# Slicing a mixer's LayerNorm and SiLU by tokens, and mixing a 31-tap convolution into its recurrence

## The reference

```
z = rmsnorm(x) @ w_in;  x_rnn, g_rnn, glu_a, glu_b = split(z, 4)          # 512 channels each
xr = conv4(x_rnn);      y_rnn = rg_lru_bidir(xr, ...) * gelu(g_rnn)       # scans over time, both ways
c = conv31(glu_a * sigmoid(glu_b));  c = silu(layernorm(c, ln_g, ln_b))   # over the 512 channels
x += concat(rmsnorm(y_rnn), rmsnorm(c)) @ w_out
x += softmax(q k^T) v @ w_xo
s = (rmsnorm(x) @ w_pq) . sub_keys      # 8 heads x 2 halves x 128 keys; top 16 of each, then of their 256 sums
x += sum_k gate_k * gelu(rmsnorm(x) . u_tab[idx_k]) * v_tab[idx_k]        # 128 picks a token
y = rmsnorm(x)
```

## Time and profile before

| | |
|---|---|
| median of three runs | 4637.21 us |
| the profiled execution | 4632.38 us, its span 4630.6 us |
| PE / DVE / POOL / ACT busy | 53% / 57% / 60% / 12% of the span |
| moved by DMA | 1497 MB, of it 1342 MB gathers |

### The profile page before, as it was taken

One profiled execution on the slowest core, in us unless ns is written; L12 is line 12 of the kernel. 1 busy time (PEld: TensorE's weight loads), 2 busy tenths in 40 slices (PEclk: granted clock), 3 DMA queues, 4 the chain that ended last, 5 costly groups with the idle time before them and its releaser, 6 DMA issues.

```text
span 4630.6 us, 30437 instructions
## 1 busy us (share of the span) xinstructions
PE 2465.1 (53%) x9492; PEld 984.2 (21%) x9492; DVE 2647.7 (57%) x5775; ACT 551.6 (12%) x1122; POOL 2763.9 (60%) x2585
## 2 busy tenths in 40 slices
PE   8996177956687444255355355355246345333354
PEld 7652132333242111011011011011012011000000
DVE  4427857688513557647657647656755755845400
ACT  6221313320210000000000000000010010000000
POOL 0003646736412366777777777777777777777754
PEclk9998588977888666577577577567668567655556
DMA  5334758969846697999999999999999999999987
GB/s 206 109 135 156 267 202 302 338 231 405 332 172 245 227 327 284 348 387 364 369 406 363 374 401 380 373 394 380 345 405 377 350 406 392 351 407 420 418 305 277
DMA packets 406466, 1496.99 MB, mean 323 GB/s; under 512 B 44576, under 2 KB 49056, under 8 KB 397856
## 3 DMA queue, kind: packets, MB, share of 16 engines
q0 software_dynamic: 368640, 1342.34, 76.6%
q1 hardware_dynamic: 31008, 144.30, 8.2%
q10 hardware_dynamic: 6656, 8.39, 0.5%
HBM read 1463.40 MB, written 31.46 MB: 323 GB/s over the span
## 4 chain that ended last, share of the span: by engine, by line
POOL 36%; PE 16%; DVE 16%; issue 14%; DMA 14%; ACT 3%; DVEq 1%; ACTq 0%; POOLq 0%; SPq 0%
POOL arena L572 20%; POOL arena L556 16%; DMA arena<-in_u,IDX 9%; DVE arena L1156 5%; PE ps L1521 4%; DMA arena<-in_v,IDXT 4%; PE ps L1640 3%; DVE arena L1087 3%; PE ps L1654 2%; PE ps L1691 2%; PE ps L1543 1%; PE ps L1556 1%; DVE arena L1205 1%; DVE CI L1211 1%; DVE CI L1202 1%
## 5 line engine op out<-in xcount | busy, mean ns | idle before, releaser
L556 POOL DMA_INDIRECT arena<-in_u,IDX x1280 | 1421.5, 1111 | 1198.5 <-DVE arena L1156 507.7
L1156 DVE SCALAR_TENSOR_TENSOR arena<-arena 128x1024 f32<-128x1024 f32 x1280 | 1546.3, 1224 | 1025.8 <-DMA arena<-in_u,IDX 1015.6
L1654 PE MATMUL ps<-arena,ZB 128*32 128x512 f32 x5120 | 1005.0, 926 | 1770.5 <-DMA arena<-in_v,IDXT 1765.2
L572 POOL DMA_INDIRECT arena<-in_v,IDXT x1280 | 1340.0, 1047 | 651.1 <-issue 381.3
L1654 PEld LDWEIGHTS ps<-arena,ZB 128*32 128x32 f32 x5120 | 200.2, 145 | 2488.1 <-issue 2471.2
L1691 PE MATMUL ps<-arena 128*128 128x512 f32 x1216 | 563.2, 619 | 13.3 <-DVE arena L1285 8.9
L1691 PEld LDWEIGHTS ps<-arena 128*128 128x128 f32 x1216 | 237.1, 200 | 356.8 <-issue 341.6
L1521 PE MATMUL ps<-arena 128*128 128x512 f32 (+1 forms) x768 | 284.0, 529 | 4.8 <-ACT arena L666 2.6
L863 ACT ACTIVATE ZB<-ACTT 128x4 f32<-128x4 f32 x320 | 58.5, 205 | 1786.7 <-PE ps L1654 1781.2
L1087 DVE SCALAR_TENSOR_TENSOR arena<-arena,cols 128x256 f32<-128x256 f32 (+1 forms) x240 | 212.2, 884 | 6.5
L1521 PEld LDWEIGHTS ps<-arena 128*128 128x128 f32 x768 | 145.7, 192 | 143.1 <-issue 134.4
(11 more groups left out here) (176 smaller groups left out, 1900.6 us busy)
## 6 DMA issues: line engine op xcount, KB each, us to landing
arena<-in_items SPq DMA_DIRECT2D x56, 1024.0 KB, 4.8
arena<-in_u,IDX POOLq DMA_INDIRECT x1280, 6.3
arena<-in_v,IDXT POOLq DMA_INDIRECT x1280
arena<-x_scratch SPq DMA_DIRECT2D x18, 512.0 KB, 6.7
arena<-in_w_out SPq DMA_DIRECT2D x16, 512.0 KB, 9.5
wp_scratch<-arena SPq DMA_DIRECT2D x2, 4096.0 KB, 17.8
arena<-wp_scratch SPq DMA_DIRECT2D x8, 1024.0 KB, 4.8
arena<-wp_scratch SPq DMA_DIRECT2D x2, 4096.0 KB, 30.4
```

The lines of the kernel that those rows point to most:

```text
L556: g.indirect_dma_start(out=u_slot[n % RU], out_offset=None, in_=a["u"], in_offset=bass.IndirectOffsetOnAxis(ap=IDX[b % 2][:, k:k + 1], axi ...
L572: g.indirect_dma_start(out=v_slot[group % VG * GROUP + quad], out_offset=None, in_=a["v"], in_offset=bass.IndirectOffsetOnAxis(ap=IDXT[b % ...
L1156: v.scalar_tensor_tensor(out=u_slot[n % RU], in0=u_slot[n % RU], scalar=1.0, in1=H[b % 2], op0=ALU.mult, op1=ALU.mult, accum_out=DOT[b % 2 ...
L1654: ins = t.matmul(ACC[b % 2][32 * quad:32 * quad + 32, half * BANK:(half + 1) * BANK], ZB[:, z + quad * ZW:z + quad * ZW + 32], v_slot[n % ...
```

## The change

`CHUNKS` puts the four g chunks ahead of the first b chunk. In both groups the taps go into the recurrence: after each step of `lru` and of the later `conv4`s up to three taps (`TAPS_EACH`) of channels already gated are issued, and what is left follows. LayerNorm and SiLU go by `SLICES` of tokens: the prompt is one slice, the sample five (128, 256, 256, 256, 128). Slice 1 stands ahead of `mix_out(m1, 0)`, slices 2 to 5 beside block 2's attention and scores, and the `mix_out`s of blocks 3 to 9 behind them, from the route of block 2 on. The four channels of a slice go through one DVE instruction; ln_g and ln_b move from DVE to ACT. For the prompt ACT does all of SiLU between two of PE's jobs. Ahead of the sample, block 1's route and block 0's dots are put in another order: nine instead of 18 dots ahead of `keep_index(0)`, three after each of ten norm steps, twelve with each head quarter, the rest among the first steps of the sample's mixer. After `mix_out(m1, 0)` PE takes groups by three ahead of each attention step, where it took two.

```diff
-CHUNKS = [("x", 0), ("x", 1), ("x", 2), ("x", 3), ("g", 0), ("b", 0), ("a", 0), ("g", 1),
-          ("b", 1), ("a", 1), ("g", 2), ("b", 2), ("a", 2), ("g", 3), ("b", 3), ("a", 3)]
+CHUNKS = [("x", 0), ("x", 1), ("x", 2), ("x", 3), ("g", 0), ("g", 1), ("g", 2), ("g", 3),
+          ("b", 0), ("a", 0), ("b", 1), ("a", 1), ("b", 2), ("a", 2), ("b", 3), ("a", 3)]
...
-SUMS_AT = ((22, 24, 30), (8, 26, 30))
-ACTS0_AT, ROUTE1_AT = 8, 5
-Z_GROUPS, B_GROUPS = 16, 36
-DOTS_FROM, DOTS_TO = 6, 190
+RNN_AT = (22, 8)
+SLICE0_AT = (24, 26, 32)
+ACTS0_AT, ROUTE1_AT = 14, 7
+Z_GROUPS = 13
+DOTS_FROM, DOTS_TO = 6, 180
+TAPS_EACH = 3
+SLICES = [(0, 0, 256), (1, 0, 128), (1, 128, 256), (1, 384, 256), (1, 640, 256), (1, 896, 128)]
...
-    last = SUMS_AT[1][2]
-    if n <= last:
-        return Z_GROUPS + (TT - Z_GROUPS) * n // last
-    return TT + (B_GROUPS - TT) * (n - last) // (len(B_JOBS) - last)
+    return Z_GROUPS + (TT - Z_GROUPS) * n // (len(B_JOBS) - 1)
+def slice_of(m, b):
+    return max(i for i, (g, lo, _) in enumerate(SLICES) if g == m.g and lo <= b * P)
...
-            sp.wait_ge(conv_summed, 1 + 1)
+            sp.wait_ge(conv_ready, 2 * CH)
             sp.dma_start(VO, flat(vo_d)).then_inc(vo_load, 16)
...
+            def center_squares(i):
+                act.wait_ge(cen_ready, i + 1)
...
+            def deviation(i):
...
+                act.activation(deviations(i), stat_bank(i, 1)[:, 0:SLICES[i][2]], ACT.Sqrt, bias=eps).then_inc(sd_ready, 1)
+            def silu(i):
+                act.wait_ge(cn_ready, i + 1)
+                for c in range(CH):
+                    ins = act.activation(ts4(i)[:, c, :], xp4(i)[:, c, :], ACT.Tanh, scale=half_lng[:, c:c + 1],
+                                         bias=half_lnb[:, c:c + 1])
+                link(ins)
+                for c in range(CH):
+                    ins = act.activation(xp4(i)[:, c, :], xp4(i)[:, c, :], ACT.Identity, scale=col("ln_g", c),
+                                         bias=col("ln_b", c))
+                ins.then_inc(ct_ready, 1)
...
+                    if m.g == 0:
+                        if n == SLICE0_AT[0] + 1:
+                            center_squares(0)
+                        if n == SLICE0_AT[1] + 1:
+                            deviation(0)
+                            silu(0)
+                            silu_squares(0)
+                        if n == SLICE0_AT[2] + 1:
+                            conv_roots(0)
+                    else:
+                        spread_to(min(b_groups(n) + 3, TT))
...
+            def mixer(m, tick):
+                def with_taps(c):
+                    def both():
                         tick()
...
-            def mixer(m, tick):
+                        taps_to(m, min(TAPS31 * c, tapped[m.g] + TAPS_EACH), tick)
+                    return both
...
                 conv4(m, 0, tick)
                 conv4(m, 1, tick)
                 for c in range(CH):
-                    lru(m, c, 0, tick)
+                    lru(m, c, 0, with_taps(c))
                     glu(m, c, tick)
+                    lru(m, c, 1, with_taps(c))
                     if m.g == 1 and c == 0:
+                        dots_to(PICKS)
                         scale_acts(0)
-                    lru(m, c, 1, tick)
                     if c + 2 < CH:
-                        conv4(m, c + 2, tick)
...
+            def center(i):
+                x, n = xp4(i), SLICES[i][2]
+                v.wait_ge(mean_done, i + 1)
+                mean = stat_bank(i, 0)[:, 0:n].unsqueeze(1).to_broadcast([P, CH, n])
+                v.tensor_tensor(x, x, mean, ALU.subtract).then_inc(cen_ready, 1)
+            def scale(i):
+                x, n = xp4(i), SLICES[i][2]
+                v.wait_ge(sd_ready, i + 1)
+                link(v.reciprocal(deviations(i), deviations(i)))
+                v.wait_ge(csq_ready, i + 1)
+                v.tensor_tensor(x, x, deviations(i).unsqueeze(1).to_broadcast([P, CH, n]), ALU.mult).then_inc(cn_ready, 1)
+            def glue(i):
+                x = xp4(i)
+                v.wait_ge(ct_ready, i + 1)
+                v.scalar_tensor_tensor(x, ts4(i), 1.0, x, ALU.add, ALU.mult).then_inc(cs_ready, 1)
+            def roots(i):
+                m = groups[SLICES[i][0]]
+                if i < 2:
+                    v.wait_ge(rnn_rooted, i + 1)
+                    v.reciprocal(rr[:, m.first:m.first + m.nb], rr[:, m.first:m.first + m.nb])
+                v.wait_ge(srt_ready, i + 1)
+                link(v.reciprocal(conv_rr(i), conv_rr(i)))
...
                 ticks[0] += 1
+                if picked[0] < PICKS:
+                    dots_to(min(picked[0] + 3, PICKS))
                 share = (ticks[0] - DOTS_FROM) / (DOTS_TO - DOTS_FROM)
-                dots_to(PICKS + int(PICKS * min(max(share, 0), 1)))
+                if picked[0] >= PICKS:
+                    share = int(PICKS * min(max(share, 0), 1))
+                    if reached[0] < len(JOBS):
+                        share = min(share, GROUP * (z_groups(reached[0]) + 2))
+                    dots_to(PICKS + share)
...
-            dots_to(12)
-            top16(0, 2)
...
+            dots_to(7)
+            norm2(1)
+            dots_to(9)
             h2(1)
-            cand_top(6)
-            experts(0, 3)
+            choose(0, 3)
             gate_in(0)
-            keep_index(0)
-            dots_to(24)
             v.wait_ge(s_done, 2 * Q)
             v.wait_ge(wp_store, 32)
             for c in range(CH):
...
-                    experts(1, q)
+            keep_index(0)
+            for i in range(m1.nb + MB):
+                recip_rstd(m1, i)
+                dots_to(9 + 3 * (i + 1))
+            for q in range(Q):
+                top16(1, q)
+                dots_to(39 + 12 * q + 4)
+                cand_top(2 * q)
+                dots_to(39 + 12 * q + 8)
+                experts(1, q)
+                dots_to(39 + 12 * q + 12)
             gate_in(1)
             keep_index(1)
             v.wait_ge(m1.xn_ready, m1.nb + MB)
@@ -1433,29 +1527,51 @@
                 v.memset(m1.CI[c][:, 0:A31], 0.0)
                 ins = v.memset(m1.CI[c][:, A31 + m1.T:], 0.0)
             link(ins)
-            dots_to(PICKS)
             mixer(m1, tick)
+            center(1)
+            dots_to(2 * PICKS)
+            scale_acts(1)
+            scale(1)
+            glue(1)
+            roots(1)
...
+            center(2)
+            scale(2)
+            final_gain(0)
+            glue(2)
             row_max(2)
-            final_gain(0)
+            roots(2)
+            probs(2)
+            center(3)
+            scale(3)
+            glue(3)
+            add_attention(2)
+            norm2(2)
+            roots(3)
+            h2(2)
+            center(4)
+            scale(4)
+            glue(4)
+            roots(4)
+            choose(2, 0)
+            center(5)
+            scale(5)
+            glue(5)
+            choose(2, 1)
+            roots(5)
             mix_out(m1, 1)
-            probs(2)
+            choose(2, 2)
             mix_out(m1, 2)
-            add_attention(2)
-            h2(2)
-            for q in range(Q):
-                top16(2, q)
-                cand_top(2 * q)
-                experts(2, q)
-                mix_out(m1, 3 + q)
-                if q >= 2:
-                    dots_to(2 * PICKS + 4 * (q - 1))
+            choose(2, 3)
             gate_in(2)
             keep_index(2)
-            mix_out(m1, 7)
+            mix_out(m1, 3)
+            for i in range(4, m1.nb):
+                dots_to(2 * PICKS + 6 * (i - 3))
...
+            def means(i):
+                g, lo, n = SLICES[i]
+                m = groups[g]
+                t.wait_ge(conv_ready, CH * (g + 1))
+                t.wait_ge(rnn_rooted, g + 1)
+                if i >= 2:
+                    t.wait_ge(ss3, 1)
                 for c in range(CH):
-                    t.wait_ge(ready, CH * m.g + c + 1)
-                    for lo, size in m.tiles:
...
@@ -1830,28 +1957,42 @@
                 z_job(m1, n)
             t.wait_ge(m1.act_took, taken(m1, len(JOBS), "act"))
             t.wait_ge(m1.dve_took, taken(m1, len(JOBS), "dve"))
-            mixer_tail(m1, SUMS_AT[1])
-            acc_to(TT + 2)
+            mixer_tail(m1)
+            means(1)
+            variances(1)
+            conv_sums(1)
             mix_out(m1, 0)
-            acc_to(TT + 4)
+            acc_to(TT + 3)
             turn_x(2)
+            means(2)
             scores(2, 0)
+            variances(2)
             scores(2, 1)
-            mix_out(m1, 1)
+            conv_sums(2)
             acc_to(TT + 6)
             turn_probs(2)
+            means(3)
             attended(2, 0)
+            variances(3)
             attended(2, 1)
-            mix_out(m1, 2)
-            acc_to(TT + 8)
+            conv_sums(3)
+            acc_to(TT + 9)
             turn_x2(2)
-            score_streamed(2)
-            for q in range(4):
```

(29 more changed lines are left out.)

269 lines of the change are left out of this document (131 added, 138 removed).

## The result

The changed kernel is slower by 0.2 to 0.6%: 4655.89 us median against 4644.01 of the kernel before, ratio 1.0042 with a 95% interval of 1.0023 to 1.0062. The ratio goes by all eleven executions of each kernel; the two medians alone would give 1.0026. Its profiled execution took 4654.83 us with a span of 4653.0, so the two spans differ by 22.4 us.

The account below looks back on a forecast made before the run. The steady stage was taken as bound by DMA bytes and unchanged, so only its earlier start counts. Chain terms summed to -21 us: 4637.2 - 21 = 4616, own range 4585 to 4640, 8-in-10 range 4555 to 4665.

Parts of the forecast that it names:

- G: Block 2's first picks to the steady stage: 159 instead of 177 us, dot 24 at 1587, then the weight load costs 15.
- C: Sample's recurrence: starts at 686 instead of 716, ends at 978 instead of 950, but with 94 taps done.
- D: Stream of remaining gathers behind the sample's recurrence: 240 us, until 1219, first sum of slice 1 at 1227 instead of 1204.
- A: Prompt, up to its mix_out: later by 32 us, from g chunks moved ahead, mixed-in taps and ACT's SiLU work.
- B: Hand-over of block 0's picks: 17 us earlier against the prompt's delay, so at 466.
- E: LayerNorm before the sample's first mix_out: 17 us instead of 86, so mix_out starts at 1244 instead of 1290.
- F: Sample's first mix_out to block 2's first picks: 184 instead of 156 us, with four PE waits for v gathers totalling 44.
- The reload: 8 MB load of wp (score weights) behind the last mix_out and dot 24 of block 2: costs about 15 us.
- The two signs: Forecast is wrong if the gather stream ends well before or after 1219, or if PE's four v-gather waits are absent.
- R2: Rival, chance 0.20: TensorE's clock falls below 0.61 in the sample's recurrence, so PE decides; slower, 4670 us.
- R1: Rival, chance 0.25: PE's v-gather waits are hidden, the wp load overlaps and the gather stream is shorter; 4551 us.
- R3: Rival, chance 0.15: the gather stream or the wp load takes up the rest, so the change misses the end; 4637 us.

Follow-up runs that it names:

- 2: Changed kernel with the prompt's taps put behind its recurrence again, the sample's taps still mixed in: ratio 0.9989 to the kernel before the change.
- 4: Changed kernel with the sample's 124 taps put behind its recurrence again, the prompt's still mixed in: ratio 0.9891 to the kernel before the change.
- 7: Changed kernel with one v group ahead of each of the last two mix_outs: ratio 1.0047 to the kernel before; with score-weight reload also cut to 1 MB, 1.0003.
- 3: Changed kernel with two instead of three v groups ahead of each block 2 attention step, the rest behind later mix_outs: ratio 0.9983 to the kernel before.

## Why the prediction was wrong

The forecast was 21 us less and the spans show 22 more: the time lies within the wide range of 4555 to 4665, but outside the forecast's own 4585 to 4640 and on the other side of the kernel before. In size it is the last term of G that failed most, then the end of C and D; in kind it is C.

A, forecast +32: the prompt's `mix_out` starts 33 us later (214.5 to 247.4). Right in size, and 2 shows that the taps are 22 of it.

B, forecast 466: 460.7. Right.

C, forecast 686 to 978: 679 to 994. The start holds. Channels 1 to 3 took 255 us instead of 239, with 92 taps done. Here lies the step that failed in kind. I counted 93 taps that go from behind the recurrence as won, and the 29 us later end as their price, and let the stream of D give it back. What the taps do to the gathers stood at nothing in that: in the recurrence each tap holds dots, and so slots (4). The recurrence took 314 us with taps and 211 without, and the stage up to the last dot 548 instead of 477. The sum took D from bytes and so had the outcome in it, but never what the same stage would be without mixing; with that I should have forecast the mixing as a loss of its own. I also took 73 dots of block 1 as done at 950 before; the trace has 64. And I did not read what the earlier trace rows meant: its row of taps without a dot held every gather (4), so a win lay in putting dots among those taps and not in moving them.

D, forecast 1219 and the first sum at 1227: last dot at 1227.4, first sum at 1239. That the end is only 8 us off is in part luck: C ended 16 late, and the stream was 7 shorter than forecast (234 for 241). Missed were the eight taps that stand behind the last dot, 10.5 us on DVE, the last 4.88 of them a wait of PE in the row of 1239.19.

E, forecast 17: 18. F, forecast 184: 192, with the four waits (38.8 for 44) as told. G, forecast 159: 164.5 to dot 24.

The reload, the last term of G, forecast at 15: this is the term that was furthest off. The way from dot 24 to the steady stage cost 31 (8.5 ahead become 22.4 behind), and only half of the cause was named. The other half, at nothing in the sum, is GpSimd's v gather, which waits 14.65 us for PE behind the last `mix_out`; with both stops gone 27.5 us go (7).

Added up from `mix_out`'s start on, the terms were short by 13 (C and D), 8 (F), 5 (G) and 16 (the reload and the stop), 42 in all, from -21 to +22. Each term was a count of work, and each left out a hand-over between queues. The two signs that were to show the forecast wrong did not come: the stream ended near 1219 and F's waits were there. None was named for the term that was furthest off.

R2's clock did fall, to a mean of 0.80 in the recurrence where 0.94 stood, but not below the 0.61 that R2 asked for, and PE was busy for 161 of 258 us. PE waited for DVE there and DVE not for PE (4), so the clock did not decide. R1's hidden waits did not come: all four of F stand in the trace. R3's slack is not there either: 2, 3 and 4 each move the end.

## What to carry to other kernels

Work put into the waits of one engine is free only if nothing that others wait for stands behind it in that engine's queue: here dots behind taps held the slots of the gathers. Ask first under what the work lay before; work that runs beside a full DMA costs little there, and moved to where DMA has to be fed it is a loss. In the old place, too, it must not lie in one piece with nothing for DMA among it. And when a stop has two causes, take both away before saying that neither matters.
